# Two trunk layers, attention heads: the row of query blocks runs on from one head into the next

## The reference, cut to what matters

```python
kvu = (ckv @ w_ukv).reshape(B, Lk, N_HEADS, NOPE_DIM + V_DIM)
k_nope, v = kvu[..., :NOPE_DIM], kvu[..., NOPE_DIM:]
def block(args):                       # one block of 128 queries, all heads
    qn_b, qr_b = args
    s = (jnp.einsum('bqhd,bkhd->bhqk', qn_b, k_nope)
         + jnp.einsum('bqhr,bkr->bhqk', qr_b, k_rope))
    p = jax.nn.softmax(s.astype(jnp.float32) * ATTN_SCALE, axis=-1).astype(v.dtype)
    return jnp.einsum('bhqk,bkhd->bqhd', p, v)
o = lax.map(block, (qn, qr))
return o.swapaxes(0, 1).reshape(B, Lq, N_HEADS * V_DIM) @ w_o
```

## Time and profile before

| | us |
|---|---|
| median of 3 runs | 3544.51 |
| lowest and highest | 3543.28, 3547.61 |
| the profiled execution's own time | 3545.17 |
| its span, first to last instruction | 3543.6 |
| mean granted TensorE clock | 0.958 of full speed |
| TensorE busy | 3278.3 (93%) |
| VectorE busy | 1806.1 (51%) |
| ScalarE busy | 940.3 (27%) |

### The profile page before, as it was taken

One profiled execution on the slowest core, in us unless ns is written; L12 is line 12 of the kernel. 1 busy time (PEld: TensorE's weight loads), 2 busy tenths in 40 slices (PEclk: granted clock), 3 DMA queues, 4 the chain that ended last, 5 costly groups with the idle time before them and its releaser, 6 DMA issues.

```text
span 3543.6 us, 48384 instructions
## 1 busy us (share of the span) xinstructions
PE 3278.3 (93%) x18847; PEld 3162.1 (89%) x18847; DVE 1806.1 (51%) x3033; ACT 940.3 (27%) x1275; POOL 163.8 (5%) x201
## 2 busy tenths in 40 slices
PE   7899999997999999999879889898978999999997
PEld 4799999996999999999779778778778999999996
DVE  7766887877333333333744555555554333333333
ACT  4222211113211111111412455454543111111114
POOL 3000000002000000000400000000000000000002
PEclk8899999998999999999889999999988999999998
DMA  5344342330111111111103100010100111111111
GB/s 204 123 146 131 104 124 93 103 108 24 42 42 41 41 43 46 38 45 39 42 26 117 66 20 27 26 35 13 32 13 24 45 44 40 43 41 41 41 42 60
DMA packets 272683, 210.41 MB, mean 59 GB/s; under 512 B 15102, under 2 KB 243756, under 8 KB 272572
## 3 DMA queue, kind: packets, MB, share of 16 engines
q1 hardware_dynamic: 260908, 163.50, 15.2%
q0 software_dynamic: 11664, 45.39, 3.6%
HBM read 185.10 MB, written 23.76 MB: 59 GB/s over the span
## 4 chain that ended last, share of the span: by engine, by line
PE 81%; DVE 10%; ACT 5%; issue 3%; DMA 1%; SPq 0%; POOL 0%; ACTq 0%; DVEq 0%; POOLq 0%
PE set L545 68%; PE set L990 4%; PE set L978 3%; PE turned L728 2%; ACT tmp L1053 2%; DVE soft L2298 1%; PE set L622 1%; DVE tmp L1767 1%; ACT pr L1053 1%; DVE hlo L1776 1%; PE set L963 1%; DVE ptl L2314 1%; PE set L951 1%; DVE pah L1889 1%; DVE x L1744 1%
## 5 line engine op out<-in xcount | busy, mean ns | idle before, releaser
L545 PE MATMUL set<-hhi,whi 128*128 128x384 f32 x2856 | 660.9, 339 | 11.4 <-DVE wlo L1661 6.2
L545 PE MATMUL set<-hlo,whi 128*128 128x384 f32 x2856 | 655.4, 337 | 0.0
L545 PE MATMUL set<-hhi,wlo 128*128 128x384 f32 x2856 | 653.9, 336 | 0.0
L1965 DVE SCALAR_TENSOR_TENSOR x<-set,mod,x 128x128 f32<-128x128 f32 x744 | 413.3, 611 | 299.9 <-PE set L545 299.9
L545 PEld LDWEIGHTS set<-hhi,whi 128*128 128x128 f32 x2856 | 514.9, 191 | 14.0 <-issue 8.4
L545 PEld LDWEIGHTS set<-hlo,whi 128*128 128x128 f32 x2856 | 515.8, 190 | 0.0
L545 PEld LDWEIGHTS set<-hhi,wlo 128*128 128x128 f32 x2856 | 514.4, 190 | 0.0
L1661 DVE TENSOR_TENSOR wlo<-wraw,whi 128x1024 fp32r<-128x1024 f32 x207 | 252.0, 1219 | 469.0 <-ACT whi L1053 439.4
L1053 ACT ACTIVATE whi<-wraw 128x1024 fp32r<-128x1024 f32 x207 | 217.4, 1052 | 708.6 <-PE set L545 701.4
L1053 ACT ACTIVATE tmp<-set 128x1152 f32<-128x1152 f32 x97 | 109.9, 1133 | 843.4 <-PE set L545 834.0
L545 PE MATMUL set<-ghi,whi 128*128 128x384 f32 x1296 | 295.0, 335 | 6.2 <-ACT tmp L1053 6.2
(11 more groups left out here) (233 smaller groups left out, 4165.7 us busy)
## 6 DMA issues: line engine op xcount, KB each, us to landing
wraw<-in_f_w_in SPq DMA_DIRECT2D x176, 256.0 KB, 3.0
adu<-in_ada_w SPq DMA_DIRECT2D x48, 512.0 KB, 6.1
wraw<-in_f_w_out SPq DMA_DIRECT2D x88, 256.0 KB, 2.7
wraw<-in_a_w_in SPq DMA_DIRECT2D x64, 256.0 KB, 4.4
v_scratch<-vst POOLq DMA_DIRECT2D x16, 576.0 KB, 3.0
vld<-v_scratch POOLq DMA_DIRECT2D x16, 576.0 KB, 4.5
q_scratch<-tmp POOLq DMA_DIRECT2D x16, 576.0 KB, 3.5
aldr<-in_ada_w SPq DMA_DIRECT2D x8, 1024.0 KB, 11.8
```

The costliest lines, as they stand in the source:

```text
L545: last = nc.tensor.matmul(ps[:, b, 0:cols], w, m[:, b * cols:(b + 1) * cols], start=(i == 0 and p == 0), stop=(i == n - 1 and p == 2))
L1965: last = v.scalar_tensor_tensor(dst, src, k.mod[:, gate + n, c:c + 1], dst, ALU.mult, ALU.add)
```

## The change

The nine blocks of a head and those of the next become one row. Rounds 7, 8 and 0 of the row issue the scores of the next head's first three jobs, so the two jobs that held only `weighted` are gone (34 jobs a pair become 30). The next head's keys are computed in round 6, before the transposes of round 6; ScalarE and VectorE do the next head's queries and keys there, ahead of the copies of those transposes, and VectorE now takes the queries before the keys. The next pair's values lie between the two halves of the output jobs. The two halves of a pair's key and value weights share slot 1 of `whi`/`wlo` (two splits of 512 columns), the output weights have slot 0; their splits move into rounds 1 to 3 of head 1. The loop has three passes instead of four, and what is left of a pair stands before and after it.

```diff
 # SyncE
+        kv_units(0)
+        with repeat(self.eng, HEADS // 2 - 1, (self.U, 4)) as i:
+            kv_units(i + 1)
             self.out_unit(d["b_w_o"][0], 2 * P * i, 0)
             self.out_unit(d["b_w_o"][0], 2 * P * i, 1)
 # TensorE
+    def next_head_ready(self):
+        k, J = self.k, self.J
+        self.G.step()
+        self.eng.wait_ge(k.q_ready, self.G.at())
+        self.eng.wait_ge(k.freed[J.odd(-1)], J.half(-1) + 1)
+    def head_round(self, h, s, before=True, ahead=True):
+        if s == 7:
+            self.turn_probs(6, True, 0)
+            self.turn_probs(7, False, 1)
+            if ahead:
+                self.next_head_ready()
+        elif s == 8 and not ahead:
+            self.turn_probs(7, True, 0)
+        if ahead or s == 8:
+            ps = self.open()
+        if ahead:
+            last = self.scores(ps, (s + 3) % 9, s - 1 if 0 < s < 7 or s == 8 else None)
+        if s % 2 == 0 and (s or before):
+            self.probs_turned()
+            last = self.weighted(ps, h if s else 1 - h, s // 2 - 1 if s else None)
+        if ahead or s == 8:
+            self.close(last)
+    def head_rest(self, h, ahead=True):
+        for s in range(1, 9):
+            self.head_round(h, s, True, ahead or s < 7)
+            if s == 6 and ahead:
+                if h == 1:
+                    self.unit_ready()
+                self.keys_job(1 - h)
+            if s != 7:
+                self.turn_probs(s, False, 1)
+            self.B.step()
 # TensorE, heads(): the loop
+            self.head_rest(0)
+            self.head_first(1, True)
+            self.head_rest(1)
+            self.head_first(0, True)
+            self.O.step(10)
+            pe.wait_ge(k.o_ready, self.O.at())
+            self.pair_out(2)
+            self.values_job(range(0, 6))
+            self.values_job(range(6, 11))
+            self.pair_out(3)
 # ScalarE
+    def head_rest(self, h):
+        for s in range(1, 6):
+            self.head_round(h, s)
+            if h == 1 and s < 3:
+                self.kv_split(s - 1)
+            if h == 1 and s == 3:
+                self.o_split()
+        self.exponentials(8, 3)
+        self.queries_hi()
+        self.keys_hi()
+        self.read_out(h, 2)
+        self.turned(6, False)
+        self.turned(6, True)
+        self.turned(7, False)
+        self.normalise(8, 3)
+        self.B.step()
+        self.exponentials(0, 3)
+        self.turned(7, True)
+        self.normalise(0, 3)
+        self.B.step()
+        self.head_round(h, 8)
+    def last_head(self):
+        for s in range(1, 6):
+            self.head_round(1, s)
+            if s < 3:
                 self.split()
 # VectorE
+    def kv_split(self, half):
+        k, s = self.k, self.U.odd()
+        self.U.step()
+        self.eng.wait_ge(k.hi_done, self.U.at())
+        lo = half * 512
+        self.nc.vector.tensor_tensor(k.wlo[:, KV_SLOT, lo:lo + 512], k.wraw[:, s, 0:512],
+                                     k.whi[:, KV_SLOT, lo:lo + 512], ALU.subtract).then_inc(k.lo_done, 1)
+    def head_first(self, h, before):
+        self.maxima(2, 3, CTX if before else 0)
+        self.turned(0, False)
+        self.inverse_sum(3)
+        if before:
+            self.out_lo(1 - h, None)
+    def head_rest(self, h):
+        for s in range(1, 6):
+            self.head_round(h, s)
+            if h == 1 and s < 3:
+                self.kv_split(s - 1)
+            if h == 1 and s == 3:
+                self.o_split()
+        self.maxima(8, 3, 2 * P)
+        self.inverse_sum(3)
+        self.queries_lo()
+        self.keys_lo()
+        self.out_lo(h, 2)
+        self.turned(6, False)
+        self.turned(6, True)
+        self.turned(7, False)
 # ScalarE and VectorE, heads(): the same loop, with values_hi/values_lo and o_split between the output halves;
 # VectorE's heads() begins with
+        self.queries_lo()
+        self.keys_lo()
+        self.values_lo()
```

More of the change, by code:

```diff
@@ new lines, in heads @@
+    def heads(self):
+        k, a, J = self.k, self.eng, self.J
+        self.queries_hi()
+        self.keys_hi()
+        self.values_hi()
+        for s in range(2):
+            self.exponentials(s, s + 1)
+            self.normalise(s, s + 1)
+        self.head_first(0, False)
+        self.turned(0, True)
+        self.normalise(2, 3)
+        self.B.step()
+        with repeat(a, HEADS // 2 - 1, (J, 30), (self.U, 4), (self.T, 50), (self.G, 2),
+                    (self.B, 18), (self.O, 10), (self.F, 10)):
+            self.head_rest(0)
+            self.head_first(1, True)
+            self.turned(0, True)
+            self.normalise(2, 3)
+            self.B.step()
+            self.head_rest(1)
+            self.head_first(0, True)
+            self.normalise(2, 3)
+            J.step(4)
+            self.o_split()
+            self.values_hi()
+            J.step(4)
+            self.turned(0, True)
+            self.B.step()
+        self.head_rest(0)
+        self.head_first(1, True)
+        self.turned(0, True)
+        self.normalise(2, 3)
+        self.B.step()
+        self.last_head()
@@ L1603, in turned @@
         k, T = self.k, self.T
-        if s % 2 == 0 and s >= 2 and not rest:
-            self.eng.wait_ge(k.mm_done, self.J.at(1))
         for g, end in prob_groups(s, rest):
@@ L2206, in queries @@
         J.step(2)
-        self.split()
+        if last:
+            self.kv_split(0)
+            self.kv_split(1)
+        else:
+            self.split()
         for h in range(2):
```

347 lines of the change are left out of this document (199 added, 148 removed).

## The result

| | before | after |
|---|---|---|
| median of 4 runs, us | 3543.9 | 3580.72 |
| lowest and highest, us | 3542.2, 3547.61 | 3577.02, 3584.26 |
| span of the profiled execution, us | 3543.6 | 3576.8 |
| mean granted TensorE clock | 0.958 | 0.953 |
| ratio of the times, 95% interval | | 1.0097 [1.0085, 1.011] |

The kernel is 1.0% slower. The forecast was 3576 us in a range of 3555 to 3592, slower. The spans of the two profiled executions differ by 33.2 us, the medians by 36.8; the forecast's sum was 31.7.

The account below looks back on a forecast made before the run. TensorE was taken as the bound, with gains only in its waits and clock. Terms 4.0 + 17.4 + 5.7 + 3.0 + 1.6 = 31.7 us on 3545.17 gave 3576.9, as median 3576 us; range 3555 to 3592.

Parts of the forecast that it names:

- within a pair, four: Third `weighted` of a head to the next head's first: 37.6 us against 36.6, four times, +4.0 us.
- across pairs, three: The same stretch with outputs and values between: 76.4 us against a mean of 70.6, three times, +17.4 us.
- weight splits, late and last head: Splits delay VectorE's next maximum: 1.9 us after round 2, three times (+5.7), and +3.0 once in the last head.
- start: VectorE does the first queries before the keys, so the keys' PSUM set is free later: +1.6 us.
- last pair's end and behind: The end of the last pair was taken as unchanged: 0.
- Round 6 and the long waits: After the next head's keys, TensorE's transposes wait 4.9 us for VectorE's copies behind queries and keys, at seven head changes.
- clock term: Lower granted clock after the 4.9 us wait within a pair: 2.0 us, between bounds of 1.3 and 4.2.
- the first split: First half of key and value weights, split after round 1 while TensorE does `weighted`: hidden, no cost.
- The table load: ScalarE's table load at the loop's turn, mid-row, 1.28 us between copies 1.7 us apart: hidden, no drain.
- Clock heavier: Rival: each of ten new long waits costs 1.4 us more clock, 3.0 to 3.4 each: 3590 us, chance 0.12.
- Clock free: Rival: new long waits replace the short ones and cost no further clock, minus 18.8: 3557 us, chance 0.11.
- Faster: Rival: round 6 copies are ready at 4.7 us instead of 9.6, removing seven waits: 3528 us, chance 0.05.

Follow-up runs that it names:

- f1_after_fill: The changed kernel with 34 added matmuls that nobody reads in each of the seven long waits behind the keys: 3559.01 us, 1.0037 of the kernel before.
- b_fill: The kernel before with matmuls that nobody reads put in front of its own short waits in the head loop: 3517.93 us, ratio 0.9921.
- e2_unrolled: The changed kernel with VectorE's loop over pairs written out, TensorE's and ScalarE's loops kept: 3570.12 us, 1.0069 of the kernel before.
- e1_splits: The changed kernel with its weight splits moved behind odd rounds in head 1 and the last head: 3564.75 us, 1.0053 of the kernel before.
- e3_queries: The changed kernel with the queries' parts handed from ScalarE to VectorE piece by piece, order unchanged: 3558.29 us, 1.0033 of the kernel before.
- e4_values: The changed kernel with the next pair's first values job moved ahead of the first half of the output jobs: 3560.71 us, 1.0039 of the kernel before.
- e5_keys_first: The changed kernel with keys before queries in round 6 on ScalarE and VectorE: 3580.88 us, 1.01 of the kernel before.

## Why the prediction was right

The direction and the main mechanism hold, and so does the size: 31.7 us were forecast, 33.2 measured between the spans, and of the terms inside the heads (4.0 + 17.4 + 5.7 + 3.0 = 30.1) the trace shows 30.1. Part by part the agreement is less good; errors of both signs cancelled, and that the total fits this well is luck. (The marks are taken from the timelines; they lie up to 0.1 us from the windows of the earlier trace rows.)

| term | forecast | measured | |
|---|---|---|---|
| within a pair, four | +4.0 | -1.3 | 36.75, 36.81, 35.48, 35.87: 144.9 against 146.2 |
| across pairs, three | +17.4 | +19.5 | 231.2 against 211.7 |
| weight splits, late and last head | +8.7 | +11.9 | inner parts of the eight heads, 248.1 against 236.2 |
| start | +1.6 | +1.3 | first `weighted` 2008.55, 2009.85; from the first keys' matmul to it 48.23 and 49.88, +1.65 |
| last pair's end and behind | 0 | +1.8 | 941.0 us and 942.8 behind the heads; 938.7 to 939.0 in five other kernels with the same orders there |

**Round 6 and the long waits: right.** 4.9 us forecast, 4.56 and 4.64 measured; 0.9 before `weighted` of round 8, measured 0.81 or 0.82. Making VectorE's queue shorter by 2.14 us of idling shortened the wait by 1.3, making it longer raised it to 6.95.

**Within a pair: the path was over-sized.** At full clock the path was put at 35.6 us, and `f1_after_fill`, which keeps the kernel's waits at a clock of 1.00, shows 34.5 three times and 34.8. So 1.1 us too much, a third of it the long wait. Its clock term, 2.0, was about right: measured is the difference of the means, 36.2 less 34.6, 1.6. So a path that was put too long made +1.0 of what was -0.3 for one passage. At full clock the passage is in fact shorter than before, 34.6 against the 35.3 of `b_fill`.

**Across pairs: a term was missing.** The forecast mean was 76.4 us, the measured 77.1. The wait at the outputs was forecast at 4.2 and is 4.04. What was missing is the turn of VectorE's loop. The prediction took the 0.76 us of TensorE's own turn from the earlier trace rows and did not ask what the turn costs the other engines; in the kernel before VectorE's turn fell where VectorE waited for the keys' copy anyway (3.47 us in the earlier trace rows). Now it falls between two rounds: `e2_unrolled` took 6 us off, 3.3 and 2.7 from the two turns that show it. Without the turn the three passages are 13.5 us above before, where 17.4 were forecast: the path was over-sized here too, and the missing term hid it.

**The splits: a term was missing.** The second split's wait is 1.49 where 1.9 was forecast, the last head's 2.82 where 3.0 was. But the first split, called hidden, shows a wait of 0.56 in the round before, and the clock behind these waits was not counted at all: 3 x 0.56 + 3 x 1.49 + 2.82 = 9.0 of the 11.9. `e1_splits` gave 11.8 back in the heads, 13.6 of them in the inner parts; the passages took 1.8 more.

**The table load: wrong place.** It was forecast in the middle of a row at each turn, hidden. The trace after has none in any pass. It loads once, ahead of the first exponential:

```profile
1995.31 1.28 ACT L1106 ACT_TABLE_LOAD   x1 [3.39 <-DVE soft L2526]
1996.61 1.33 ACT L1106 ACTIVATE pr<-set,soft 128x1280 f32<-128x1280 f32 x1
...
1998.08 0.85 PE L984 MATMUL set<-kth,qnh 128*128 128x512 f32 x3 [1.19 <-ACT pr L1106]
```

There it isn't hidden: TensorE waits 1.19 us for the exponential behind it. So the size of the start's term was right and its cause half wrong. Counted from the first keys' matmul, which starts 0.37 us earlier in the trace of after, the first `weighted` comes 1.65 us later. The values' wait ends 1.0 us later by the same count (1984.50 in the earlier trace rows, 1985.16 now), not 1.6, although it lasts 16.91 us instead of 9.98: it begins some 6 us earlier, 4.2 of them because the values no longer wait for `wlo` first, as they did before. The other 0.6 us lie behind the values, where the exponential behind the table load is waited for. The Trainium skill ("ScalarE: Activation LUTs", What ACT_TABLE_LOAD costs) adds a drain of some 1380 ns to the load; here as in the earlier trace rows the next ScalarE instruction starts at once, 0.02 us after the load's end.

**The last pair's end: 0 forecast, +1.8 found, and not the code's.** In the last head ScalarE does the small exponential before the copies of job 6, and TensorE's waits at the end are 1.89, 0.33, 1.02, 0.84 and 1.10 us. But `e1_splits`, `e3_queries`, `e4_values`, `e5_keys_first` and `f1_after_fill` have the same order there and waits within 0.2 us of these, and from the last head's third `weighted` to the end of the output matmuls they take 58.8 us, where the kernel after took 61.4 and before 59.6. What differs is the clock, 27.5 us at the lower level in the trace of after against 20. So the 1.8 us is the chance of one trace; what the order of the last head costs is not shown.

**The rivals.** Clock heavier (3.0 to 3.4 for each long wait) is refuted for the waits at the keys by `f1_after_fill`: 1.6 each at the place, 2.7 at most. The three waits at the outputs were not filled. Clock free is refuted as a number (3557) and half right as a mechanism: a passage within a pair pays 1.6 us of clock now and paid 1.3 before (36.6 less 35.3), so there the long wait did take the place of the short ones. The splits were not absorbed. Faster, by transposes that get past the queries, is refuted by VectorE's rows, which stand as written. What the prediction did not see is the other side: the kernel before pays for its clock in the inner parts too. `b_fill`, which leaves no lower clock in its heads, gave them 20.9 us back for 58 us at the lower level; filling seven waits gave 18.6 to those of after for 51 of their 85 us. At that price per us the whole 85 would cost some 30 us, an estimate, so the clock would be some 10 us of the 30.1 between the two kernels. It is the smaller part either way; TensorE's idle time grew by 26.6.

**What stays open.** Where the low-clock stretches fall. They can be read in each trace, and on them hang both the missing part of the four repairs' sum and the time of `e5_keys_first`, with 16.5 us more of waits and no slower; but what moves them from run to run was not tried. A difference of 2 to 4 us between two single traces is therefore no measure of an edit, wherever the rows don't show it at its place. The last head's end was not tried by itself.

## What to carry to other kernels

When work is moved to an earlier place so that TensorE always has something to issue, look at what it passes on the engines that execute in written order: here the next head's queries and keys stood ahead of the one copy that TensorE needed, and the wait of 2.8 us at a head's end became one of 4.6 a little earlier. Then go on: with four local orders put right (splits in rounds that have slack, pieces handed over one by one, an independent job ahead of a wait, no loop turn in the middle of a pipeline) the same change was worth 0.5% instead of costing 1%. And look at an unchanged stretch of the traces before crediting an edit with its whole time: here such a stretch differed by 4 us. And compare two structures with their waits filled, once: it tells what is clock and what is order, and here it also gave the cheapest gain, 0.8% on the kernel before without any change of its order.

## What the runs showed of the hardware

**Short waits lower the clock too.** In the kernel before, no wait inside the heads is longer than 2.85 us, and yet its granted clock falls to 0.5 sixteen times between 1990 and 2623 us; one of these falls is shown in the result's section, behind the wait of 2.85. With added matmuls (268 recorded there, 39.2 us of TensorE's time, most of it where it idled) it does not fall once in the same stretch:

```profile
1990.00:2623.00 633.00, 591.13 (x3800) 528.43 (x3798) 370.79 (x674) 337.07 (x541) 12.89 (x24) 1.00 0.08 24
```

The Trainium skill ("TensorE: Matmul & The Clock Gate", A second HAM failure mode: psum-queue depth-cycling) tells of a kernel whose TensorE idles briefly and often between groups of matmuls, swings between the two levels and pays for it. These traces agree, and show in addition that matmuls nobody reads stop it: 0.8% of this kernel's time.

**A loop's turn on VectorE cost 2.70 and 2.53 us** of idling that nothing in the profile explains, where it did not fall beside a wait of its own, and with VectorE's loop written out this idling is gone (0.32 us behind TensorE); TensorE's turns in the same kernel cost at most 0.6 us.
